# Neighbourhood attention with all queries and keys projected first and its heads' scores in pairs, reordered steps in the even layer, and two constants loaded over another queue

## What is computed

```python
def neighbourhood_attention(h, w_qkv, w_o, rel_bias):      # 16 heads of 64
    qkv = (h @ w_qkv).reshape(b, rows, GRID_W, 3, N_HEADS, HEAD_DIM)
    ...
    scores = jnp.where(col_mask, q_r @ k_band + bias, NEG_INF)
    p = jax.nn.softmax(scores, axis=(-2, -1))
    o = jnp.einsum('bhjqrk,bhrjkd->bhjqd', p, v_band)
    return out @ w_o
def nsa_compress(a, pe, w1, w2):
    hid = jax.nn.silu(jnp.einsum('bnlgd,lde->bnge', blocks, w1))
    return jnp.einsum('bnge,ef->bngf', hid, w2)
def even_layer(...):
    gates = jax.nn.sigmoid(ng + gate_b)
    ...   # compressed, selected and windowed attention, MoBA, memory attention
    y = concatenate([a_out * silu(nz), b_out * silu(mz), m_out * silu(ez)]) @ w_out
def reference(...):
    x = attention, peer mixer, convolution mixer, peer mixer      # first block
    return even_layer, odd_layer, rms_norm                         # second block
```

## Time and profile before

| what | value |
|---|---|
| median of 3 runs | 2384.48 us |
| lowest, highest | 2381.69, 2386.47 us |
| the profiled execution: its own time | 2386.18 us |
| its span, first to last instruction | 2384.3 us |
| mean granted clock of TensorE | 0.993 of full speed |
| busy: TensorE, VectorE, ScalarE | 98%, 71%, 56% of the span |

### The profile page before, as it was taken

One profiled execution on the slowest core, in us unless ns is written; L12 is line 12 of the kernel. 1 busy time (PEld: TensorE's weight loads), 2 busy tenths in 40 slices (PEclk: granted clock), 3 DMA queues, 4 the chain that ended last, 5 costly groups with the idle time before them and its releaser, 6 DMA issues.

```text
span 2384.3 us, 45063 instructions
## 1 busy us (share of the span) xinstructions
PE 2337.2 (98%) x15648; PEld 2096.6 (88%) x15648; DVE 1688.2 (71%) x3190; ACT 1332.5 (56%) x2506; POOL 44.1 (2%) x87
## 2 busy tenths in 40 slices
PE   8999999999999999999999999999999998899998
PEld 7889999999988888899999999988888887788776
DVE  5656996899755555675898799956556577667565
ACT  4545545777655555445455677755554455665554
POOL 1000000000000000000000000000000000000000
PEclk9999999999999999999999999999999999999999
DMA  7445666444566666565565544566666653246454
GB/s 234 124 141 156 177 187 179 143 142 142 169 193 194 194 194 192 161 185 187 168 179 182 160 143 142 157 196 192 202 195 178 183 175 100 71 125 197 129 159 141
DMA packets 137082, 397.44 MB, mean 167 GB/s; under 512 B 12321, under 2 KB 13521, under 8 KB 136177
## 3 DMA queue, kind: packets, MB, share of 16 engines
q1 hardware_dynamic: 134432, 384.97, 53.6%
q0 software_dynamic: 2512, 10.66, 1.3%
HBM read 394.54 MB, written 1.05 MB: 166 GB/s over the span
## 4 chain that ended last, share of the span: by engine, by line
PE 89%; DVE 5%; ACT 3%; issue 2%; DMA 0%; POOL 0%; DVEq 0%; ACTq 0%; POOLq 0%
PE bank L999 31%; PE bank L1015 29%; PE bank L897 12%; PE bank L903 7%; PE bank L1028 4%; PE bank L956 1%; PE bank L944 1%; ACT wh L1337 1%; DVE wl L1727 1%; PE bank L929 1%; PE bank L980 1%; DVE aux L1765 1%; PE bank L949 1%; PE bank L908 0%; ACT arena L1326 0%
## 5 line engine op out<-in xcount | busy, mean ns | idle before, releaser
L1727 DVE TENSOR_TENSOR wl<-raw,wh 128x1024 fp32r<-128x1024 f32 (+1 forms) x732 | 893.5, 1222 | 541.4 <-ACT wh L1337 530.0
L1337 ACT ACTIVATE wh<-raw 128x1024 fp32r<-128x1024 f32 (+1 forms) x732 | 771.7, 1055 | 639.8 <-PE bank L1015 337.3
L999 PE MATMUL bank<-xh,wh 128*128 128x256 f32 x2048 | 511.7, 288 | 0.0
L999 PE MATMUL bank<-xl,wh 128*128 128x256 f32 x2048 | 502.0, 283 | 0.0
L999 PEld LDWEIGHTS bank<-xl,wh 128*128 128x128 f32 x2048 | 392.9, 192 | 0.0
L999 PEld LDWEIGHTS bank<-xh,wh 128*128 128x128 f32 x2048 | 392.2, 192 | 0.5
L999 PE MATMUL bank<-xh,wl 128*128 128x256 f32 x2048 | 287.8, 283 | 0.0
L1015 PE MATMUL bank<-wh,gl 128*128 128x512 f32 x1008 | 270.1, 390 | 1.7 <-DVE gl L2109 1.7
L1015 PE MATMUL bank<-wh,gh 128*128 128x512 f32 x1008 | 269.8, 389 | 0.5 <-ACT gh L1510 0.5
L1015 PE MATMUL bank<-wl,gh 128*128 128x512 f32 x1008 | 269.4, 389 | 0.0
L999 PEld LDWEIGHTS bank<-xh,wl 128*128 128x128 f32 x2048 | 264.0, 192 | 0.9 <-DVE wl L1727 0.4
(11 more groups left out here) (295 smaller groups left out, 2695.8 us busy)
## 6 DMA issues: line engine op xcount, KB each, us to landing
raw<-in_w_upT SPq DMA_DIRECT2D x256, 512.0 KB, 3.6
raw<-in_w_down SPq DMA_DIRECT2D x256, 512.0 KB, 3.7
raw<-in_l_w_in SPq DMA_DIRECT2D x84, 512.0 KB, 3.6
raw<-in_peer_w_query SPq DMA_DIRECT2D x32, 512.0 KB, 4.2
raw<-in_l_w_out SPq DMA_DIRECT2D x28, 512.0 KB, 3.7
raw<-in_attn_w_qkv SPq DMA_DIRECT2D x24, 512.0 KB, 4.3
raw<-in_conv_w_in SPq DMA_DIRECT2D x24, 512.0 KB, 3.7
arena<-in_na_bias POOLq DMA_DIRECT2D x4, 1024.0 KB, 7.1
```

Source lines behind the costliest of these rows:

```text
L999: last = pe.matmul(banks[b][:, 0:SEQ], lhsT=w[part][:, k, :], rhs=x_in[xp][:, k, :], start=(k == 0 and part == 0 and xp == 0), stop=(k == ...
L1337: act.activation(wh[:, n % SPLIT, 0:kts * cols], raw[:, n % RAW, 0:kts * cols], ACT.Copy)\
L1727: tt(wl[:, n % SPLIT, 0:kts * cols], raw[:, n % RAW, 0:kts * cols], wh[:, n % SPLIT, 0:kts * cols].bitcast(F32), ALU.subtract).then_inc(lo ...
```

## The change

The 24 projection units come in the order q 0 to 7, k 0 to 7, q 8 to 15, k 8 to 15, then the values. S of heads 2k and 2k + 1 stand after unit 9 + 2k, T of the even head one unit and T of the odd head two units later, O of two heads after each of units 20 to 23, of four after unit 24, of two after 25 and 26. The turned weights of all 16 heads have a place of their own, and so have the sums. In ScalarE's list of a unit the T steps stand before the S steps, in all attentions. In the even layer "even_T" 6 and 8 move one unit forward, "silu" 2 moves from unit (6, 3) to (7, 3), Silu and Sigmoid of the compression and the gates become exp(-x) on ScalarE and an addition of 1, a reciprocal and (for Silu) a product on VectorE, and the copies of "kvc" are issued without a wait after each. The identity and the gains are loaded over ScalarE's queue, with a semaphore each. In the convolution mixer the row scales are transposed after unit 3.

```diff
@@ -63,11 +63,11 @@
-WO_TURN, OUT_TURN, EVEN_TURN, ROWS_AFTER, ROWS_EARLY = 30, 1, 2, 7, 2
+WO_TURN, OUT_TURN, EVEN_TURN, ROWS_AFTER, ROWS_EARLY, ROWS_CONV = 30, 1, 2, 7, 2, 3
...
-L_QT, L_KT, L_V, L_BIAS, L_O, L_OT = 0, 2048, 4096, 6144, 14336, 16384
+L_QT, L_KT, L_V, L_BIAS, L_O, L_OT, L_PT = 0, 2048, 4096, 6144, 14336, 16384, 20480
@@ -185,8 +185,8 @@
-    (4, 3): [("even_T", 6), ("even_T", 7), ("rope", 10)], (5, 0): [("rope", 11)],
-    (5, 3): [("even_T", 8), ("even_T", 9)], (6, 3): [("silu", 2)], (7, 0): [("even_T", 10)], (7, 3): [("silu", 0)],
+    (4, 2): [("even_T", 6)], (4, 3): [("even_T", 7), ("rope", 10)], (5, 0): [("rope", 11)],
+    (5, 2): [("even_T", 8)], (5, 3): [("even_T", 9)], (7, 0): [("even_T", 10)], (7, 3): [("silu", 2), ("silu", 0)],
@@ -221,13 +221,13 @@
-QKV_CHUNKS = (0, 2, 4, 1, 3, 5)
+QKV_CHUNKS = (0, 2, 1, 3, 4, 5)
...
-NA_S = tuple(9 + a if a < 8 else 21 + (a - 8) // 2 for a in range(NA_HEADS))
-NA_T = tuple(NA_S[a] + (2 if a < 8 else 1) for a in range(NA_HEADS))
-NA_O = tuple(NA_T[a] + 1 if a < 8 else max(NA_T[a] + 1, 24) for a in range(NA_HEADS))
-NA_JOINED = (17, 20, 25, 27)
+NA_S = tuple(9 + a // 2 * 2 for a in range(NA_HEADS))
+NA_T = tuple(NA_S[a] + 1 + a % 2 for a in range(NA_HEADS))
+NA_O = tuple(20 + a // 2 if a < 8 else (24, 25, 26)[max(0, a // 2 - 5)] for a in range(NA_HEADS))
+NA_JOINED = (22, 24, 26, 27)
@@ -481,7 +481,7 @@
-        norm_loaded = sem("identity_and_gains_loaded")
+        ident_loaded, gains_loaded = sem("identity_loaded"), sem("gains_loaded")
@@ -509,6 +509,7 @@
+        hid_exp = sem("hidden_exp")
@@ -537,7 +538,8 @@
-        na_s, na_pT = aux_view(0, 6, TT, SEQ), aux_view(3072, 6, 2 * TT, P)
+        na_s, na_pT = aux_view(0, 6, TT, SEQ), view(L_PT, NA_HEADS, 2 * TT, P)
+        na_sums = aux_view(3072, NA_HEADS, TT)
@@ -546,12 +548,12 @@
-            return {"na": na_pT[:, n % 6], "ev": ev_pT[:, n % 4], "om": pT_buf[:, n % 2]}[name]
+            return {"na": na_pT[:, n % NA_HEADS], "ev": ev_pT[:, n % 4], "om": pT_buf[:, n % 2]}[name]
...
-            return small[:, at:at + 2]
+            return na_sums[:, n] if name == "na" else small[:, at:at + 2]
@@ -704,9 +706,6 @@
-            pool.dma_start(ident[:], d["c_ident"]).then_inc(norm_loaded, 16)
-            pool.dma_start(gains[:], d["gains"]).then_inc(norm_loaded, 16)
-
@@ -834,7 +833,7 @@
-                        pe.wait_ge(norm_loaded, 16 * 2)
+                        pe.wait_ge(ident_loaded, 16)
@@ -1242,11 +1241,11 @@
-                        pe.wait_ge(norm_loaded, 16 * 2)
+                        pe.wait_ge(gains_loaded, 16)
...
-                        for c in (0, 1) if kind == "S" else (2,):
+                        for c in (2 * (a // 8), 2 * (a // 8) + 1) if kind == "S" else (4 + a // 8,):
...
-                                wait_read(pe, J.of("qkv", 2 * (3 * (a // 8) + c) + i))
+                                wait_read(pe, J.of("qkv", 2 * c + i))
@@ -1258,7 +1257,7 @@
-                project("qkv", "TTNTTN"[c], x_in, k=2 * c, ready=norm_parts("attn"), after=lambda u: na_unit(4 * c + u))
+                project("qkv", "TTTTNN"[c], x_in, k=2 * c, ready=norm_parts("attn"), after=lambda u: na_unit(4 * c + u))
@@ -1272,7 +1271,7 @@
-                    elif 4 * c + u == ROWS_EARLY:
+                    elif 4 * c + u == ROWS_CONV:
@@ -1400,8 +1399,9 @@
-            def attention(name, order, heads, base, some=None):
-                for kind, a in order if some is None else [order[k] for k in some]:
+            def attention(name, order, heads, base, some):
+                steps = [order[k] for k in some]
+                for kind, a in [s for s in steps if s[0] == "T"] + [s for s in steps if s[0] == "S"]:
@@ -1561,11 +1561,13 @@
-                        evac(hid_sb[0:HEAD, :, :, 0:N_CMP], j, src.rearrange("p a (g n) -> p a g n", g=2), ACT.Silu)
+                        wait_filled(act, j)
+                        act.activation(hid_sb[0:HEAD, :, :, 0:N_CMP], src.rearrange("p a (g n) -> p a g n", g=2), ACT.Exp, scale=-1.0)\
+                            .then_inc(hid_exp, 1)
...
-                        act.activation(gates, gates, ACT.Sigmoid).then_inc(nsa_gate, 1)
+                        act.activation(gates, gates, ACT.Exp, scale=-1.0).then_inc(nsa_gate, 1)
@@ -1599,6 +1601,8 @@
+            act.dma_start(ident[:], d["c_ident"]).then_inc(ident_loaded, 16)
+            act.dma_start(gains[:], d["gains"]).then_inc(gains_loaded, 16)
@@ -1610,10 +1614,10 @@
-                if n % 4 == 3 and c in (2, 5):
+                if n % 4 == 3 and c in (4, 5):
...
-                        evac(na_v[:, t, c // 3 * CHUNK:(c // 3 + 1) * CHUNK], J.of("qkv", 2 * c + t), scale=token[:, t:t + 1])
+                        evac(na_v[:, t, (c - 4) * CHUNK:(c - 3) * CHUNK], J.of("qkv", 2 * c + t), scale=token[:, t:t + 1])
@@ -2198,7 +2202,7 @@
-            dve.wait_ge(norm_loaded, 16 * 2)
+            dve.wait_ge(gains_loaded, 16)
@@ -2229,13 +2233,13 @@
-                if n % 4 == 3 and c in (0, 1, 3, 4):
+                if n % 4 == 3 and c < 4:
...
-                        j, i = J.of("qkv", 2 * c + k), 4 * (c // 3) + 2 * k
+                        j, i = J.of("qkv", 2 * c + k), 4 * (c // 2) + 2 * k
...
-                        if c in (0, 3):
+                        if c % 2 == 0:
@@ -2249,7 +2253,7 @@
-            lows(conv + ROWS_EARLY)
+            lows(conv + ROWS_CONV)
@@ -2377,7 +2381,12 @@
-                        wait_read(dve, J.of("hid"))
+                        j, hid = J.of("hid"), hid_sb[0:HEAD, :, :, 0:N_CMP]
+                        src = bank(j)[0:HEAD, 0:64].rearrange("p (a x) -> p a x", a=2)[:, :, 0:2 * N_CMP]
+                        dve.wait_ge(hid_exp, 1)
+                        step(ts(hid, hid, 1.0, None, ALU.add))
+                        step(dve.reciprocal(hid, hid))
+                        read_out(tt(hid, src.rearrange("p a (g n) -> p a g n", g=2), hid, ALU.mult), j)
@@ -2389,11 +2398,9 @@
-                        step(dve.tensor_copy(kcT[:, k, 0:N_CMP], bank(j)[:, 0:N_CMP]))
+                        dve.tensor_copy(kcT[:, k, 0:N_CMP], bank(j)[:, 0:N_CMP])
...
-                            if i < 3:
-                                step(ins)
@@ -2414,6 +2421,8 @@
+                        step(ts(gates, gates, 1.0, None, ALU.add))
+                        step(dve.reciprocal(gates, gates))
```

## The result

The changed kernel takes 2363.36 us in the median of four runs (2362.79 to 2365.95), the kernel before 2385.47 in four (2381.69 to 2386.81): a ratio of 0.9912, 95% interval 0.99 to 0.9924. The forecast was 2362. The profiled execution of the changed kernel is its longest, 2365.95, with a span of 2363.9; the other three have spans of 2360.8 to 2361.7. The mean clock went from 0.993 to 0.995.

What follows compares the result with a forecast made beforehand. TensorE, busy 2337.2 of 2384.3 us, bounds the kernel. Terms 2.2 + 4.2 + 3.5 + 5.0 + 0.8 + 7.2 - 0.6 = 22.3, taken from the median of 2384.48, give 2362; range 2355 to 2370.

Steps and rivals of the forecast that it cites:

- Two of the signs by which I would have called the prediction wrong: Identity releasing TensorE at the start; more than one clock fall in the even layer; also new waits in units 20 to 25.
- The start: Kernel start: TensorE's first transposes begin at 5.3 instead of 7.57, released by x; gain 2.2 us.
- a start that doesn't move: Rival at the start: ScalarE's queue or x is slow, 0 to 2.2 us are missing, ending at 2364; chance 0.04.
- Pairs: First layer's attention: eight heads' single scores become four pairs running beside each other; gain 4.2 us.
- The output projection's start and the clock there: First layer's attention: waits of 2.04, 1.57 and 0.17 go, gain 3.5; the slow clock from 111 to 132 goes, gain 5.0.
- Convolution mixer: Convolution mixer: TensorE's wait for GpSimd's row scale goes by placing its transposes one unit later; gain 0.8 us.
- Even layer, gains: Even layer: waits of 1.71 and 2.16 behind ScalarE's copies go, 3.9, and the clock behind them, 3.3; sum 7.2 us.
- the clock behind them: Even layer: the slow clock behind the waits of 1.71 and 2.16 goes, 1.6 + 1.7 = 3.3 us.
- dealt anew: Rival on the clock: shifted waits draw other falls, perhaps the wait of 2.64; 2367 or 2357; chance 0.12.
- Even layer, costs: Even layer: added VectorE steps cost 0.7 and 0.5, copies without waits save 0.6; together 0.6 us lost.
- late softmax: Rival in the first layer's attention: paired transposes wait for weights, up to 0.5 each, 4 in all, 2366; chance 0.08.
- slower than before: Rival in units 20 to 26: crowded outputs make TensorE wait for VectorE, 9 us slower, 2394; chance 0.02.

Runs made afterwards that it cites:

- e2: Changed kernel with the odd heads' scores one unit later, so that no unit has two (pairs undone); 2375.0 us, ratio 0.9958.
- e15: Changed kernel with the even layer's parts undone together (transposes, silu step, ScalarE's order, waited copies, Silu and Sigmoid); 2368.57 us, ratio 0.9932.
- e4: Changed kernel with TensorE's first transposes waiting for the gains too, queues unchanged; 2366.37 us, ratio 0.9921.
- e5: Changed kernel with the silu step of gate pair 2 back one slot earlier; 2364.44 us, ratio 0.9912.
- e14: Changed kernel with Silu and Sigmoid on ScalarE, even heads' scores spread, and transposes before scores on TensorE in the even attention; 2362.78 us, ratio 0.9904.
- e7: Changed kernel with ScalarE's attention steps in list order again, even_T still one by one; 2372.92 us, ratio 0.9945.
- e8: Changed kernel with even_T 6 to 9 two by two and ScalarE's attention steps in list order again; 2369.04 us, ratio 0.9937.
- e6: Changed kernel with even_T 6 to 9 two by two again, ScalarE's transposes-first order kept; 2362.03 us, ratio 0.9901.

## Why the prediction was right, and which terms were not

The time (2362 forecast, 2363.36 measured) and the main steps held. That the number is so close is in part luck. The sum forecast 22.3, the medians have 22.1 and the profile has 20.4. Against the profile the attention gave 1.3 more than its 12.7, the even layer 1.8 less than its 6.6, and the convolution mixer 1.3 less than its 0.8, by a fall of the clock there. Two of the signs by which I would have called the prediction wrong came: TensorE is released by the identity at the start, and the even layer has four falls of the clock where I allowed one. Term by term:

- **The start**, forecast 2.2, measured 2.24. The releaser was not x, as the step had it, but the identity: at 5.04 and not 3.6. TensorE's start was 0.26 earlier than the 5.3 forecast, and 0.3 of the 2.53 was lost again in the transposes, 4.01 for 3.67, probably for the second piece of x, which took 5.0 to land. The size is right by chance: the identity came 1.4 later than I had it, and TensorE began with x's first piece alone. The rival, a start that doesn't move, needed the identity still later; the trace shows 4.3 for it where I took 2.9 from a transfer on another queue.
- **Pairs**, forecast 4.2. From e2, 1.2 a pair and so 4.7 for the four new ones; the dearer first product behind each group of scores was not in the sum.
- **The output projection's start and the clock there**, forecast 3.5 and 5.0. All 3.8 of waits went, and all 10.2 us at the lower clock, 4.6 at the measured 0.45. With the pairs that is 4.7 + 3.8 + 4.6 = 13.1 of the 14.0 measured; 0.9 is not placed. The bank that I held to be late next was not late, and the 0.3 kept back for it not needed.
- **Convolution mixer**, forecast 0.8, and 1.0 measured in ten of the eleven profiles with it (70.87 to 70.89 for 71.87). The changed kernel's own profile shows +0.49, for a fall behind the wait of 1.82, worth 72.36 - 70.87 = 1.5. The step is right; the clock spoils it in that execution.
- **Even layer, gains**, forecast 7.2. The 3.9 of waits went. The term that failed is "the clock behind them", 3.3: these two falls went, 6.8 us at the lower clock, but one of 6.8 came at the wait of 3.11, and the sum is 17 us before and after. The rival "dealt anew" named this very wait and is right for this layer, and wrong for the attention, where no wait was left to draw one. I also gave the credit to three edits (the order, the transposes, the silu step), when the order alone is enough for all of it.
- **Even layer, costs**, forecast 0.6, measured 1.02 + 0.69 + 0.47 = 2.2 less some 0.4 of the copies. I priced a reciprocal by a copy of the same elements, 0.245; it took 0.52. The product behind the hidden layer waits 1.29, not the 0.9 that I gave as a sign. And I had no term for the doubled unit, where the transposes one by one add 0.43 to 0.47 once ScalarE has its new order. Waits gone less costs is 3.9 + 0.4 - 2.2 = 2.1, near the 2.6 of e15 against e4 and e5; the profile's 4.8 has the covered wait on top.

The rivals "late softmax" and "slower than before" did not happen: there is no wait over 0.15 from 15 to 133 us.

What stays open: the copies without waits and the new conv placement were not tried alone; why the spread order of e14 gains nothing; how much of the differences between medians is the clock, since each kernel has one profile; and what decides which wait draws a fall of the clock.

## What to carry to other kernels

Where one engine is busy for 98% of the span, price a change by the waits and by the work laid beside other work, and book the clock behind a wait as won only where the stage is left with no wait at all; where others remain, half of a few microseconds may go either way, and variants are compared at equal time at the lower clock, not by one median. When several edits aim at the same wait, undo each alone and both together: here one order was enough for everything, and its companion, the transposes one by one, cost 0.4 us of waits with it and 2.0 without it (e7 against e8: 4.76 and 2.75 in waits for ScalarE). A table load saved on an engine that waits anyway earned nothing here, and the steps that replaced it on another engine's path cost 1.0 us.

## What the runs showed that I had not expected

- A reciprocal on VectorE is long for its size: 0.52 for 60 elements a partition and 0.45 for 48, where the addition before each took 0.18. The Trainium skill (VectorE: DVE Perf Modes, First, the fixed hardware budget) says that the reciprocal is an iterative divide with a repeat count of 8. No run here shows the repeats; the trace shows 0.25 for a reciprocal of 16 elements, so that each element more takes some 6 ns, where the additions before the three took 0.17 to 0.18 whatever their size.
- Runs of the same start begin with TensorE at either clock: four matmuls in 1.19 or in 0.71, and the attention's stretch is 0.9 to 1.9 longer for it. The windows' column of the granted clock shows 1.00 in both (10 to 14 us, the changed kernel and e5); only the duration of the products tells. The Trainium skill (TensorE: Matmul & The Clock Gate, What's actually happening) says that the activity is judged in windows that run freely and don't start with the kernel; the trace agrees, since e5 and e6 do the same up to there and begin at different levels.
- One of the five executions of e14 had TensorE at half speed to the end: 4614.8 us in place of 2363. VectorE was busy for 1697.7 us in it and for 1690.3 in the changed kernel's profile; TensorE needed 4598.6 in place of 2327.5. Its first four products took 1.12, like the 1.19 of a start at the lower clock, but no later row shows a rise.
